# Encoder layer with mLSTM: scores, weights and scaled operands of each chunk formed beside the value projection and kept in DRAM

## Chip, cores and metric

One core of a Trainium2 chip runs the whole layer in one launch. The metric is device time in microseconds; a program's time is the median of its runs.

## The reference

1280 tokens of width 1024 in two sequences (256 and 1024 tokens, 2 and 8 chunks of 128) go through one layer, in float32. A norm and one input projection give pooled channels, and queries, keys, values, output gates and gates of an mLSTM with 4 heads of 128. It scans chunks in both directions; in one direction, per chunk and head:

```python
b = jnp.cumsum(fc, axis=-1)
logw = jnp.where(mask, b[..., :, None] - b[..., None, :] + ic[..., None, :], -jnp.inf)
m_row = jnp.maximum(b + m[..., None], jnp.max(logw, axis=-1))
s = jnp.einsum('bhjd,bhsd->bhjs', qc, kc) * jnp.exp(logw - m_row[..., None])
inter = jnp.exp(b + m[..., None] - m_row)
num = jnp.einsum('bhjs,bhsd->bhjd', s, vc) + inter[..., None] * jnp.einsum('bhed,bhjd->bhje', C, qc)
den = jnp.sum(s, axis=-1) + inter * jnp.einsum('bhd,bhjd->bhj', n, qc)
h = num / jnp.maximum(jnp.abs(den), jnp.exp(-m_row))[..., None]
# then C and n are decayed and gain u * v k and u * k
```

The heads of both directions are added, normed and gated; an output projection, a second norm, a router and 32 experts (top 2) and a last norm follow. Nothing of the latter is touched by the change.

## The kernel before

The five engines and their queues run programs of their own, ordered by semaphores; the order in each is written out by hand. The large products are made of three products of split operands (`product3`, L636 to L638).

The stages in order: norm and transposes of x; projections of 512, 512 and 256 tokens in the list `proj` (pooling, gates, output gates, keys, queries); then the values, one tile of 128 tokens at a time (`NPROJ + t`, 24 matmuls of 512 columns each); then the recurrence; then, per chunk, head norm, output projection and router; then the experts and the last norm. SP loads the slices of w_in through two slots of `w_st` (L403); each is split by ScalarE (L919) and VectorE (L1219).

The recurrence goes over `NU` = 40 units, two for each pair of heads in each of 10 steps, one for either direction `d`; `chunk_of` gives the chunk that a direction takes in a step. Per unit TensorE first does `unit_scores` for the unit after: two transposed key tiles (L728), two score tiles (L730), the mask and the negative row maximum brought into PSUM by products with selecting columns (L735, L736), and the factor of the state's part, `e_inter`, spread over the partitions in the same way (L738). ScalarE scales the keys (`uk`, L1044) and takes the exponential (`wgt`, L1052). VectorE multiplies scores and weights (`sT`, L1400) and scales the queries (`qi`, L1402). Then `unit_rows` on TensorE: state times queries and values times weighted scores (L751, L752), and what the state gains (L755, not in each sequence's last step). VectorE forms the denominator (L1413 to L1416), updates the state of two heads (L1419) and writes the pair's rows of `h_fb` (L1427). The next step of the same direction and pair is four units later. Meanwhile SP loads w_out slice by slice (L433), and ScalarE and VectorE split it after every fourth unit (L1058, L1440).

After the last unit (`h_done`, `NU`) SP loads what the output projection needs (L442 to L446). Each unit's tiles live in PSUM banks 4d to 4d + 3. GpSimd adds the two directions' h chunk by chunk (L567) and is idle otherwise.

Of the kernel before, what the change touches and what calls it, by code (L numbers as in the profile page):

```python
# [21 lines left out]
def build(nc, x_prompt, x_sample, norm1_g, w_in, pool_w, pool_scale, gate_b, head_norm_g, w_out,  # L22
# [28 lines left out]
    ogate_dram = nc.dram_tensor("ogateT", (MW, T), F32).ap()  # L51

# [18 lines left out]
    identb = const("identb", [P, P], BF16)  # L71
    maskb = const("maskb", [P, 2, P], BF16)
# [22 lines left out]
    row_picks = const("row_picks", [P, 8], F32R)  # L95
    e_inter = const("e_inter", [P, T], F32R)
    negm = const("negm", [P, T], F32R)
# [46 lines left out]
    dn = at("dn", X0 + 77 * KB, [P, 2, 2], F32)  # L144
    rdn = at("rdn", X0 + 77 * KB + 64, [P, 2, 2], F32)
    wo_lo = at("wo_lo", W0, [P, KD, D], F32R)
    uk = at("uk", V0, [P, 2, 2, P], F32)
    wgt = at("wgt", V0 + 2 * KB, [P, 2, 2, P], F32)
    sT = at("sT", V0 + 4 * KB, [P, 2, 2, P], F32)
    qi = at("qi", X0 + 77 * KB + 128, [P, 2, 2, P], F32)  # L150
# [58 lines left out]
    with ctx:  # L209
# [3 lines left out]
        def sem(name):  # L213
# [19 lines left out]
        g_abs, g_exp, g_ln, rows_ready, turned, dec_ready, cols_done, v_ones, state_zero, e_inter_exp, e_inter_hi, e_inter_done = (  # L233
            sem(n) for n in ("g_abs", "g_exp", "g_ln", "rows_ready", "turned", "dec_ready", "cols_done", "v_ones",
                             "state_zero", "e_inter_exp", "e_inter_hi", "e_inter_done"))

        kq_ready, nm_ready, uk_done, wgt_done, s_done, qi_done, kv_ready, rdn_done, state_done, h_done = (
            sem(n) for n in ("kq_ready", "nm_ready", "uk_done", "wgt_done", "s_done", "qi_done", "kv_ready", "rdn_done", "state_done", "h_done"))
# [14 lines left out]
        chosen_done, rank_ready, slots_done, count_ready, rounds_done, wexp_done, wts_done = (  # L253
            sem(n) for n in ("chosen_done", "rank_ready", "slots_done", "count_ready", "rounds_done", "wexp_done",
                             "wts_done"))
# [12 lines left out]
        f_in = [sem(f"f_in{i}") for i in range(NT)]  # L268
# [15 lines left out]
        N_CONST = 10  # L284
# [58 lines left out]

        def complete_after(t):
# [4 lines left out]
        EARLY = NT - 4  # L349

# [39 lines left out]
        def _(sp):  # L390
# [37 lines left out]
            for i in range(KD):  # L428
                if i < 2:
                    sp.wait_ge(wlo_done, NSL)  # L430
                else:
# [3 lines left out]
            for i in range(4):  # L435
                sp.wait_ge(ev_out[i], 16 * len(ring[i::4]))
            sp.wait_ge(h_done, NU)
            sp.wait_ge(state_done, NU)
# [60 lines left out]
            for t in range(NT):  # L499
                for k in range(2):  # L500
                    sp.dma_start(f_y[:, t, k, :], y_dram[k * T + t * P:k * T + (t + 1) * P, :]).then_inc(f_in[t], 16)
# [7 lines left out]
        def _(pool):  # L509
# [19 lines left out]
            for tile, value in ((identb[:, :], 0.0), (maskb[:, :, :], 0.0), (laterb[:, :], 1.0),  # L529
                                (edge[:, :, :], 1.0)):  # L530
                pool.memset(tile, value).then_inc(pool_step, 1)
            pool.wait_ge(pool_step, 5)
            pool.affine_select(out=identb[:, :], in_=identb[:, :], compare_op=ALU.not_equal, fill=1.0, base=0,
                               pattern=[[-1, P]], channel_multiplier=1).then_inc(consts_done, 1)
            for d, sign in enumerate((1, -1)):
                pool.affine_select(out=maskb[:, d, :], in_=maskb[:, d, :], compare_op=ALU.is_ge, fill=MASKED, base=0,
                                   pattern=[[sign, P]], channel_multiplier=-sign).then_inc(consts_done, 1)
# [12 lines left out]
            pool.wait_ge(pool_step, 8)  # L550
# [12 lines left out]


# [67 lines left out]
        def _(pe):  # L632
# [8 lines left out]
            def picks(r):  # L641
                return row_picks[:, r:r + 1].broadcast_to([P, P])

# [63 lines left out]

            for t in range(NT):
                n = NPROJ + t
                if t == 0:  # L710
# [10 lines left out]
            def unit_scores(n):  # L721
                step, pair, d, ck = unit(n)
                tok = slice(ck * P, (ck + 1) * P)
                heads = (2 * pair, 2 * pair + 1)
                if n >= 2:
                    pe.wait_ge(qi_done, n - 1)
                for hh_, h in enumerate(heads):
                    pe.transpose(psum[:, 4 * d, hh_ * P:(hh_ + 1) * P], kT[:, h, tok], ident[:, :])  # L728
                for hh_, h in enumerate(heads):
                    last = pe.matmul(psum[:, 4 * d, (2 + hh_) * P:(3 + hh_) * P], kT[:, h, tok], qT[:, h, tok],  # L730
                                     start=True, stop=True)
                last.then_inc(kq_ready, 1)
                for hh_, h in enumerate(heads):
                    out = psum[:, 4 * d + 1, hh_ * P:(hh_ + 1) * P]
                    pe.matmul(out, identb[:, :], maskb[:, d, :], start=True, stop=False)  # L735
# [965 lines left out]
```

## Time and profile before

| | us |
|---|---|
| median of 3 runs | 1281.9 (1279.71 to 1282.23) |
| profiled execution | 1278.36 |
| its span, first to last instruction | 1276.6 |
| PE busy | 1155.9 (91%) |
| DVE busy | 876.0 (69%) |
| ACT busy | 686.2 (54%) |
| POOL busy | 178.9 (14%) |

The profile is one execution on the chip. PE is TensorE's matmuls, PEld its weight loads, DVE VectorE, ACT ScalarE, POOL GpSimd; SPq is an issue on SP's DMA queue. Durations of matmuls are modelled and overlap, so what one costs is read from the distance between starts. PEclk is the granted TensorE clock as a share of full speed.

### The profile page before, as it was taken

Reading aid. Unit: us, or ns where it says so; the run is one execution under the profiler, and the core shown is the slowest. Engines: PE = TensorE matmul, PEld = TensorE weight load, DVE = VectorE, ACT = ScalarE, POOL = GpSimd, SP = SyncE. Lnnn points to the kernel's source line nnn. Section 1 sums busy time; section 2 is a strip of 40 time slices with the busy share of each in tenths; the row PEclk is TensorE's granted clock in tenths of the full one; section 3 lists DMA queues with packets and bytes.
Section 4 is the critical chain, followed back from the end, with each engine's and each line's share of the span. In section 5 each row is a group of like instructions: output and inputs, shape, how many; then the busy total and the mean of one; then the engine's idle time right before and its main releaser. Section 6 shows DMA issues by size and latency. Waiting matters only on the chain.

```text
span 1276.6 us, 18695 instructions
## 1 busy us (share of the span) xinstructions
PE 1155.9 (91%) x6071; PEld 978.7 (77%) x6071; DVE 876.0 (69%) x1413; ACT 686.2 (54%) x1122; POOL 178.9 (14%) x255
## 2 busy tenths in 40 slices
PE   5999999999999989998399999999999999999920
PEld 4887888878899968887278788888888888888810
DVE  5649410010188836665488999999999999999958
ACT  5431331121265643323177887788778877887733
POOL 1100200000010200212211221222122212211100
PEclk9999999999999989998599999999999999999965
DMA  8112230110011063542579999999999999999757
GB/s 229 56 45 71 101 97 17 50 60 7 1 51 51 2 197 101 106 143 100 196 266 369 366 376 384 382 375 387 385 384 384 387 385 384 375 378 388 272 228 302
DMA packets 118115, 282.05 MB, mean 221 GB/s; under 512 B 22144, under 2 KB 53376, under 8 KB 118064
## 3 DMA queue, kind: packets, MB, share of 16 engines
q1 hardware_dynamic: 103600, 245.01, 53.1%
q0 software_dynamic: 14464, 36.37, 7.6%
q8 instruction: 31, 0.51, 0.2%
q14 instruction: 20, 0.16, 0.0%
HBM read 261.76 MB, written 32.68 MB: 231 GB/s over the span
## 4 chain that ended last, share of the span: by engine, by line
PE 50%; DVE 7%; ACT 4%; DMA 2%; issue 1%; ACTq 0%; POOL 0%; SPq 0%; POOLq 0%; DVEq 0%
PE psum L636 15%; PE psum L638 15%; PE psum L637 15%; DVE e_lo L1533 3%; ACT e_hi L1105 3%; PE psum L849 2%; PE psum L807 1%; PE psum L882 1%; DVE x L1660 1%; DVE x L1668 1%; DVE x L1658 1%; PE psum L796 1%; DMA gx<-xn_scratch,row_of 1%; DMA f_y<-expert_rows 0%; PE psum L775 0%
## 5 line engine op out<-in xcount | busy, mean ns | idle before, releaser
L1533 DVE TENSOR_TENSOR e_lo<-e_st,e_hi 128x1024 fp32r<-128x1024 f32 x384 | 442.4, 1218 | 16.0 <-ACT e_hi L1105 15.1
L1105 ACT ACTIVATE e_hi<-e_st 128x1024 fp32r<-128x1024 f32 x384 | 372.3, 1050 | 9.5 <-PE psum L638 9.1
L636 PE MATMUL psum<-e_hi,ex_hi 128*128 128x512 f32 x512 | 204.3, 399 | 8.9 <-DVE ex_lo L1580 3.7
L637 PE MATMUL psum<-e_lo,ex_hi 128*128 128x512 f32 x512 | 200.8, 392 | 0.0
L638 PE MATMUL psum<-e_hi,ex_lo 128*128 128x512 f32 x512 | 200.7, 392 | 0.0
L636 PE MATMUL psum<-xT_hi,w_hi 128*128 128x512 f32 (+1 forms) x408 | 146.2, 358 | 6.4 <-DVE w_lo L1219 3.3
L638 PE MATMUL psum<-xT_hi,w_lo 128*128 128x512 f32 (+1 forms) x408 | 144.9, 355 | 0.0
L637 PE MATMUL psum<-xT_lo,w_hi 128*128 128x512 f32 (+1 forms) x408 | 144.8, 355 | 0.0
L636 PEld LDWEIGHTS psum<-e_hi,ex_hi 128*128 128x128 f32 x512 | 96.7, 189 | 42.0 <-DVE e_lo L1533 16.6
L638 PEld LDWEIGHTS psum<-e_hi,ex_lo 128*128 128x128 f32 x512 | 96.7, 189 | 20.9
L637 PEld LDWEIGHTS psum<-e_lo,ex_hi 128*128 128x128 f32 x512 | 96.8, 189 | 19.1
L1219 DVE TENSOR_TENSOR w_lo<-w_st,w_hi 128x1024 fp32r<-128x1024 f32 x21 | 25.6, 1222 | 121.3 <-ACT w_hi L919 121.3
L636 PE MATMUL psum<-e_hi,ht_hi 128*128 128x512 f32 x256 | 105.8, 413 | 1.3 <-DVE yo L1599 1.1
L638 PE MATMUL psum<-e_hi,ht_lo 128*128 128x512 f32 x256 | 100.4, 392 | 0.0
L637 PE MATMUL psum<-e_lo,ht_hi 128*128 128x512 f32 x256 | 100.0, 391 | 0.0
L636 PEld LDWEIGHTS psum<-xT_hi,w_hi 128*128 128x128 f32 x408 | 77.6, 190 | 18.0 <-DVE w_lo L1219 4.0
L638 PEld LDWEIGHTS psum<-xT_hi,w_lo 128*128 128x128 f32 x408 | 77.4, 190 | 10.9
L637 PEld LDWEIGHTS psum<-xT_lo,w_hi 128*128 128x128 f32 x408 | 77.5, 190 | 10.6
L603 POOL COPY row_to<-rows_to 128x1 int32 (+1 forms) x32 | 27.1, 848 | 416.9 <-DVE yo L1599 416.9
L636 PE MATMUL psum<-wo_hi,mix_hi 128*128 128x512 f32 x160 | 65.1, 407 | 1.2 <-DVE mix_lo L1458 1.2
L637 PE MATMUL psum<-wo_lo,mix_hi 128*128 128x512 f32 x160 | 63.2, 395 | 0.0
L638 PE MATMUL psum<-wo_hi,mix_lo 128*128 128x512 f32 x160 | 63.2, 395 | 0.0
(233 smaller groups left out, 1872.7 us busy)
## 6 DMA issues: line engine op xcount, KB each, us to landing
e_st<-in_expert_w_gate_dram SPq DMA_DIRECT2D x128, 512.0 KB, 5.8
e_st<-in_expert_w_up_dram SPq DMA_DIRECT2D x128, 512.0 KB, 6.8
e_st<-in_expert_w_down_dram SPq DMA_DIRECT2D x128, 512.0 KB, 8.6
w_st<-in_w_in_dram SPq DMA_DIRECT2D x20, 512.0 KB, 4.0
f_y<-expert_rows SPq DMA_DIRECT2D x20, 512.0 KB, 12.2
xn_scratch<-xn POOLq DMA_DIRECT2D x10, 512.0 KB, 3.4
out_dram<-x SPq DMA_DIRECT2D x10, 512.0 KB, 4.8
x_in<-in_x_sample_dram POOLq DMA_DIRECT2D x8, 512.0 KB, 5.2
```

Of the source, the lines that this page charges most:

```text
L603: pool.tensor_copy(row_to[:, b:b + 1], rows_to[:, bass.ds(i, 1)]).then_inc(row_placed, 1)
L636: pe.matmul(out, a_hi, b_hi, start=start, stop=False)
L637: pe.matmul(out, a_hi, b_lo, start=False, stop=False)
L638: return pe.matmul(out, a_lo, b_hi, start=False, stop=stop)
L796: last = pe.transpose(psum[:, 5 + k // 4, (k % 4) * P:(k % 4 + 1) * P], xn2[:, t % 2, k:D:KD], ident[:, :])
L807: last = pe.matmul(psum[:, 7, 0:NL], xn2T[:, k, :], rw[:, k, :], start=(k == 0), stop=(k == KD - 1))
L849: last = pe.transpose(psum[:, 2 + k // 4, (k % 4) * P:(k % 4 + 1) * P], gx[:, b, k:D:KD], ident[:, :])
L882: last = pe.transpose(psum[:, 6, k * P:(k + 1) * P], hh[:, k:F:KF], ident[:, :])
L1105: act.activation(e_hi[:, r, :, :], e_st[:, slot, :, :], ACT.Copy).then_inc(ehi_done, 1)
L1219: dve.tensor_tensor(w_lo[:, m % 4, :, :], w_st[:, m % 2, :, :], w_hi[:, m % 4, :, :].bitcast(F32), ALU.subtract).then_inc(wlo_done, 1)
L1533: dve.tensor_tensor(e_lo[:, r, :, :], e_st[:, slot, :, :], e_hi[:, r, :, :].bitcast(F32), ALU.subtract).then_inc(elo_done, 1)
L1658: link(dve.scalar_tensor_tensor(out=x1[:, t, :], in0=f_y[:, t, 0, :], scalar=wts[:, 0, t:t + 1], in1=x1[:, t, :], op0=ALU.mult, op1=ALU.add))
```

## The change

Scores, weights, scaled keys and scaled queries no longer belong to a unit. They are formed in 20 blocks, one for each chunk and pair of heads with both directions in it, while TensorE projects the values: two blocks' transposes and scores stand ahead of each value tile from the second on. The negative maxima and the state's factors are written to DRAM as rows, and each block's rows are read back broadcast over 128 partitions. GpSimd masks them, ScalarE adds the bias and takes the exponential, VectorE multiplies. One of three buffers `blk` holds a block (128 x 1536 floats), which SP stores in `units_dram`. The recurrence loads each unit's 128 x 768 floats from there: the first four into the place of xT_lo, the others into eight slots that lie over qT and kT. A unit on TensorE is `unit_rows` alone, with four banks for rows and four for gains; units of a sequence's first step leave the state product out. ScalarE writes `h_fb`; VectorE's small steps are laid between its state updates. Columns of the gates are formed before the first keys are taken. The constants for masking and selecting by TensorE go.

```diff
     ogate_dram = nc.dram_tensor("ogateT", (MW, T), F32).ap()
+    negm_dram = nc.dram_tensor("neg_max_rows", (2 * H, T), F32).ap()
+    inter_dram = nc.dram_tensor("inter_rows", (2 * H, T), F32).ap()
...
+    blk = [at(f"blk{i}", off, [P, 2, 3, 2, P], F32) for i, off in enumerate((V0, top_rows, W0 + 32 * KB))]
+    first_units = at("first_units", X0 + 40 * KB, [P, KD, T], F32)
+    units = at("units", Q0, [P, 8, 6, P], F32)
...
+            def block_in(i):
+                ck, pair = BLOCKS[i]
+                tok = slice(ck * P, (ck + 1) * P)
+                if i == 0:
+                    sp.wait_ge(rows_out, 64)
+                    for j in range(4):
+                        sp.wait_ge(ev_out[j], 16 * len(ring[j::4]))
+                elif i == 2:
                     sp.wait_ge(wlo_done, NSL)
...
+                elif i >= 3:
+                    sp.wait_ge(blk_out[i % 3], 16 * (i // 3))
+                for kind, rows, arrived in ((0, negm_dram, nm_in), (2, inter_dram, inter_in)):
+                    for d in range(2):
+                        sp.dma_start(blk[i % 3][:, d, kind, :, :],
+                                     rows[d * H + 2 * pair:d * H + 2 * pair + 2, tok].unsqueeze(0)
+                                     .broadcast_to([P, 2, P])).then_inc(arrived[i % 3], 16)
+            def block_out(i):
+                sp.wait_ge(s_done, i + 1)
+                sp.dma_start(units_dram[i].rearrange("p d n -> p (d n)"),
+                             blk[i % 3][:, :, :, :, :].rearrange("p d k h n -> p (d k h n)")).then_inc(blk_out[i % 3], 16)
+            def unit_load(n):
+                step, pair, d, ck = unit(n)
+                if n >= 12:
+                    sp.wait_ge(kv_ready, n - 7)
+                dst = first_units[:, 0:6, n * P:(n + 1) * P] if n < 4 else units[:, n % 8, :, :]
+                sp.dma_start(dst, units_dram[BLOCKS.index((ck, pair)), :, d, :]
+                             .rearrange("p (k n) -> p k n", n=P)).then_inc(unit_in[n % 8], 16)
+            def wo_in(i):
+                if i >= 2:
                     sp.wait_ge(wolo_done, i - 1)
                 sp.dma_start(w_st[:, i % 2, :, :].rearrange("p k n -> p (k n)"),
                              w_out[0, i * P:(i + 1) * P, :]).then_inc(wo_load[i % 2], 16)
...
+            for i in range(3):
+                block_in(i)
+            for i in range(NB):
+                block_out(i)
+                if i + 3 < NB:
+                    block_in(i + 3)
+                if i == NB // 2:
+                    sp.wait_ge(proj_ready, NPROJ + 4)
+                    for n in range(4):
+                        unit_load(n)
+            for j in range(3):
+                sp.wait_ge(blk_out[j], 16 * len(range(j, NB, 3)))
+            for n in range(4, 12):
+                unit_load(n)
+                if n == 4:
+                    wo_in(0)
+                    wo_in(1)
+            for n in range(12, NU):
+                unit_load(n)
+                if n % 4 == 0 and 2 <= n // 4 - 1 < KD:
+                    wo_in(n // 4 - 1)
...
+            for i in range(NB):
+                pool.wait_ge(nm_in[i % 3], 32 * (i // 3 + 1))
+                for d, sign in enumerate((1, -1)):
+                    logw = blk[i % 3][:, d, 0, :, :]
+                    ins = pool.affine_select(out=logw, in_=logw, compare_op=ALU.is_ge, fill=MASKED, base=0,
+                                             pattern=[[0, 2], [sign, P]], channel_multiplier=-sign)
+                ins.then_inc(masked, 1)
...
+            def block_scores(i):
+                ck, pair = BLOCKS[i]
+                tok = slice(ck * P, (ck + 1) * P)
+                if i == 0:
+                    pe.wait_ge(cols_done, 1)
+                    pe.wait_ge(act_took, act_results(NPROJ))
+                if i >= 4:
+                    pe.wait_ge(s_done, i - 3)
+                for hh_ in range(2):
+                    pe.transpose(psum[:, 4 + i % 4, hh_ * P:(hh_ + 1) * P], kT[:, 2 * pair + hh_, tok], ident[:, :])
+                for hh_ in range(2):
+                    last = pe.matmul(psum[:, 4 + i % 4, (2 + hh_) * P:(3 + hh_) * P], kT[:, 2 * pair + hh_, tok],
+                                     qT[:, 2 * pair + hh_, tok], start=True, stop=True)
+                last.then_inc(kq_ready, 1)
             for t in range(NT):
                 n = NPROJ + t
+                for i in range(max(2 * t - 1, 0), 2 * t + 1 + (t == NT - 1)):
+                    block_scores(i)
...
+                pe.wait_ge(unit_in[n % 8], 16 * (n // 8 + 1))
+                if n >= 4:
+                    pe.wait_ge(h_done, n - 3)
+                    pe.wait_ge(state_done, states_kept(n - 3))
+                for hh_ in range(2):
+                    h = 2 * pair + hh_
+                    out = psum[:, n % 4, hh_ * (P + 1):(hh_ + 1) * (P + 1)]
+                    if not from_zero(step):
+                        pe.matmul(out, unit_part(n, 2, hh_), state[:, d, h, :], start=True, stop=False)
+                    last = pe.matmul(out, unit_part(n, 0, hh_), v[:, ck, h, :], start=from_zero(step), stop=True)
                 if carries(step):
...
+                    for hh_ in range(2):
+                        last = pe.matmul(psum[:, 4 + n % 4, hh_ * (P + 1):(hh_ + 1) * (P + 1)], unit_part(n, 1, hh_),
+                                         v[:, ck, 2 * pair + hh_, :], start=True, stop=True)
                 last.then_inc(kv_ready, 1)
...
+            pe.wait_ge(s_done, NB)
...
+                        act.activation(inter_rows[0:64, :], g_e[:, :], ACT.Exp).then_inc(inter_done, 1)
+                        gate_columns()
...
+            def block_weights(i):
+                ck, pair = BLOCKS[i]
+                act.wait_ge(masked, i + 1)
+                for d in range(2):
+                    for hh_ in range(2):
+                        r = d * H + 2 * pair + hh_
+                        wgt = blk[i % 3][:, d, 0, hh_, :]
+                        ins = act.activation(wgt, wgt, ACT.Exp, bias=cols[:, ck, 0, r:r + 1])
+                ins.then_inc(wgt_done, 1)
+            block_weights(0)
+            for t in range(NT):
+                for i in range(2 * t + 1, min(2 * t + 3, NB)):
+                    block_weights(i)
+                v_part(t)
...
+                act.wait_ge(rdn_done, n + 1)
                 for hh_ in range(2):
...
+                    h = 2 * pair + hh_
+                    ins = act.activation(h_fb[:, d, ck, h * P:(h + 1) * P],
+                                         psum[:, n % 4, hh_ * (P + 1):hh_ * (P + 1) + P], ACT.Copy,
+                                         scale=rdn[:, n % 4, hh_:hh_ + 1])
+                ins.then_inc(h_done, 1)
...
+            def block_products(i):
+                ck, pair = BLOCKS[i]
+                tok = slice(ck * P, (ck + 1) * P)
+                keys = psum[:, 4 + i % 4, 0:2 * P].rearrange("p (h n) -> p h n", h=2)
+                scores = psum[:, 4 + i % 4, 2 * P:4 * P].rearrange("p (h n) -> p h n", h=2)
+                dve.wait_ge(inter_in[i % 3], 32 * (i // 3 + 1))
+                dve.wait_ge(kq_ready, i + 1)
+                qi = blk[i % 3][:, :, 2, :, :]
+                for d in range(2):
+                    dve.tensor_tensor(qi[:, d, :, :], qi[:, d, :, :], qT[:, 2 * pair:2 * pair + 2, tok], ALU.mult)
+                for d in range(2):
+                    r = d * H + 2 * pair
+                    dve.tensor_tensor(blk[i % 3][:, d, 1, :, :], keys,
+                                      cols[:, ck, 2, r:r + 2].unsqueeze(2).broadcast_to([P, 2, P]), ALU.mult)
+                dve.wait_ge(wgt_done, i + 1)
+                for d in range(2):
+                    ins = dve.tensor_tensor(blk[i % 3][:, d, 0, :, :], scores, blk[i % 3][:, d, 0, :, :], ALU.mult)
+                ins.then_inc(s_done, 1)
+            for i in range(NB):
+                block_products(i)
...
+                def keep(hh_):
+                    old = state[:, d, 2 * pair + hh_, :]
+                    return dve.scalar_tensor_tensor(out=old, in0=old, scalar=decay[:, r + hh_, step:step + 1],
+                                                    in1=gained[:, hh_, :], op0=ALU.mult, op1=ALU.add)
+                wait(dve, h_done, n - 3)
+                steps[0] += 2
+                dve.tensor_tensor(dn[:, n % 4, :], num[:, :, P], cols[:, ck, 1, r:r + 2], ALU.max).then_inc(dve_step, 1)
+                if carries(step) and from_zero(step):
+                    dve.tensor_copy(state[:, d, 2 * pair:2 * pair + 2, :], gained).then_inc(state_done, 1)
+                elif carries(step):
+                    keep(0)
+                dve.wait_ge(dve_step, steps[0] - 1)
+                dve.scalar_tensor_tensor(out=dn[:, n % 4, :], in0=num[:, :, P], scalar=-1.0, in1=dn[:, n % 4, :],
+                                         op0=ALU.mult, op1=ALU.max).then_inc(dve_step, 1)
+                if carries(step) and not from_zero(step):
+                    keep(1).then_inc(state_done, 1)
+                dve.wait_ge(dve_step, steps[0])
+                dve.reciprocal(rdn[:, n % 4, :], dn[:, n % 4, :]).then_inc(rdn_done, 1)
```

## Rows read from the trace of the kernel before

**Rows 1.** Windows: stretch, busy time of each engine, clock, DMA share, GB/s.

```profile
284.00:340.20 56.20, 56.20 (x240) 46.04 (x240) 0.00 (x0) 6.41 (x25) 0.00 (x0) 0.97 0.05 19
...
341.70:444.20 102.50, 101.66 (x920) 100.72 (x920) 84.98 (x311) 63.02 (x217) 12.67 (x8) 1.00 0.09 32
```

**Rows 2.** Timeline of one unit: start us, us, engine, line, operation.

```profile
370.80 0.38 PE L728 MATMUL psum<-ident,kT 128*128 128x128 f32 x2
...
371.00 0.16 DVE L1413 TENSOR_TENSOR dn<-psum,cols 128x2 f32<-128x2 f32 x1
371.02 0.61 PE L730 MATMUL psum<-qT,kT 128*128 128x128 f32 x4
371.20 0.16 DVE L1414 SCALAR_TENSOR_TENSOR dn<-psum,dn 128x2 f32<-128x2 f32 x1
...
371.47 0.22 PE L735 MATMUL psum<-maskb,identb 128*128 128x128 bf16 x1
...
371.48 0.59 DVE L1419 SCALAR_TENSOR_TENSOR state<-state,decay,psum 128x129 f32<-128x129 f32 x2
...
372.05 0.44 PE L751 MATMUL psum<-state,qi 128*128 128x129 f32 x2
...
372.99 0.61 PE L755 MATMUL psum<-v,uk 128*128 128x129 f32 x4
...
373.44 0.38 PE L728 MATMUL psum<-ident,kT 128*128 128x128 f32 x2
```

**Rows 3.** Groups of instructions from 200 to 560 us: busy us, mean ns.

```profile
L1052 ACT ACTIVATE wgt<-psum,cols 128x128 f32<-128x128 f32 x80 | 25.0, 364 | 0.0
...
L1400 DVE TENSOR_TENSOR sT<-psum,wgt 128x256 f32<-128x256 f32 x40 | 16.9, 423 | 14.6 <-ACT wgt L1052 14.2
...
L1440 DVE TENSOR_TENSOR wo_lo<-w_st,wo_hi 128x1024 fp32r<-128x1024 f32 x8 | 9.7, 1215 | 0.0
...
L1058 ACT ACTIVATE wo_hi<-w_st 128x1024 fp32r<-128x1024 f32 x8 | 8.4, 1055 | 0.0
```

**Rows 4.** Timeline of the SP queue's issues after the last h.

```profile
446.72 0.38 SPq L442 DMA_DIRECT2D mixf<-pooledT  x1
447.15 0.50 SPq L444 DMA_DIRECT2D og<-ogateT  x1
447.70 0.50 SPq L446 DMA_DIRECT2D x<-in_x_prompt_dram  x1
```

**Rows 5.** Issues of L504: landing, us from issue.

```profile
DMA to landing us min/median/max: 2.6/4.8/15.3
```

**Rows 6.** Windows: the experts' stage, columns as in the first group.

```profile
610.00:1230.00 620.00, 584.55 (x2706) 478.06 (x2706) 543.38 (x563) 451.39 (x541) 116.12 (x133) 0.97 0.94 353
```

**Rows 7.** Issues of L403, slices of w_in: landing.

```profile
DMA to landing us min/median/max: 3.7/4.0/9.7
```

**Rows 8.** Issues of L433, slices of w_out: landing.

```profile
DMA to landing us min/median/max: 3.1/3.2/4.3
```

**Rows 9.** The issue of L407, norm1_g broadcast: landing.

```profile
DMA to landing us min/median/max: 5.2/5.2/5.2
```

**Rows 10.** Groups of GpSimd.

```profile
L520 POOL TENSOR_SCALAR_AFFINE_SELECT ident<-ident 128x128 f32<-128x128 f32 x1 | 0.3, 284 | 0.2 <-POOL ident L518 0.2
```

**Rows 11.** Timeline before the value projection.

```profile
282.67 1.23 DVE L1219 TENSOR_TENSOR w_lo<-w_st,w_hi 128x1024 fp32r<-128x1024 f32 x1 [1.13 <-ACT w_hi L919]
...
283.92 0.84 SPq L433 DMA_DIRECT2D w_st<-in_w_out_dram  x2
```

**Rows 12.** Timeline of VectorE in the gate rows.

```profile
103.05 3.05 DVE L1345 SCALAR_TENSOR_TENSOR negm<-g_m,negm 32x1280 fp32r<-32x1280 f32 x3
```

**Rows 13.** Windows: clock around the first output projection.

```profile
449.00:450.00 1.00, 0.35 (x2) 0.00 (x0) 0.00 (x0) 0.44 (x2) 0.13 (x1) 0.50 1.44 332
...
457.00:458.00 1.00, 1.00 (x4) 0.71 (x4) 0.38 (x2) 0.00 (x0) 0.00 (x0) 0.50 1.08 342
...
459.00:460.00 1.00, 1.00 (x5) 0.78 (x5) 0.12 (x1) 1.00 (x3) 0.00 (x0) 1.00 0.63 231
```

More of the change, by code:

```diff
@@ L341, in unit, with states_kept @@
             return step, pair, d, chunk_of(step, d)
+        def states_kept(n):
+            return sum(carries(m // 4) for m in range(n))
         def complete_after(t):
@@ L349, in build, with from_zero @@
         EARLY = NT - 4
+        BLOCKS = [(c, pair) for c in sorted(range(NT), key=lambda c: min(s for s in range(NT) for b in range(2)
+                                                                          if chunk_of(s, b) == c)) for pair in range(2)]
+        NB = len(BLOCKS)
+        def from_zero(step):
+            return step in (0, C0)
         def carries(step):
@@ L717, in _ @@
                 last.then_inc(proj_ready, 1)
[L721 to L735, printed above, removed]
-                    pe.matmul(out, picks(d * H + h), negm[:, tok], start=False, stop=True)
-                for hh_, h in enumerate(heads):
-                    last = pe.matmul(psum[:, 4 * d + 1, (2 + hh_) * P:(3 + hh_) * P],
-                                     picks(d * H + h), e_inter[:, tok], start=True, stop=True)
-                last.then_inc(nm_ready, 1)
@@ L742, in unit_rows @@
             def unit_rows(n):
                 step, pair, d, ck = unit(n)
-                heads = (2 * pair, 2 * pair + 1)
-                pe.wait_ge(qi_done, n + 1)
-                if n >= 2:
-                    pe.wait_ge(h_done, n - 1)
-                    pe.wait_ge(state_done, n - 1)
-                for hh_, h in enumerate(heads):
-                    out = psum[:, 4 * d + 2, hh_ * (P + 1):(hh_ + 1) * (P + 1)]
-                    pe.matmul(out, qi[:, d, hh_, :], state[:, d, h, :], start=True, stop=False)
-                    last = pe.matmul(out, sT[:, d, hh_, :], v[:, ck, h, :], start=False, stop=True)
+                pe.wait_ge(unit_in[n % 8], 16 * (n // 8 + 1))
@@ L997, in _, with v_part @@
                 take(n)
[L1000 to L1012 removed]
+            def v_part(t):
                 act.wait_ge(proj_ready, NPROJ + t + 1)
@@ L1343, in gate_rows_stabilised @@
                 dve.wait_ge(list_set, 16)
[L1344 to L1350 removed]
+                by_direction(lambda r, o, i: dve.tensor_scalar(negm_rows[r, o], g_m[r, i], -1.0, None, ALU.mult))
                 dve.tensor_tensor(chunked(g_i), per_chunk(mprev), chunked(g_m), ALU.subtract)
@@ L1417, in heads_out @@
-                if carries(step):
-                    for hh_ in range(2):
-                        ins = dve.scalar_tensor_tensor(
-                            out=state[:, d, 2 * pair + hh_, :], in0=state[:, d, 2 * pair + hh_, :],
-                            scalar=decay[:, r + hh_, step:step + 1],
-                            in1=psum[:, 4 * d + 3, hh_ * (P + 1):(hh_ + 1) * (P + 1)], op0=ALU.mult, op1=ALU.add)
-                else:
-                    ins = dve.memset(state[:, d, 2 * pair:2 * pair + 2, :], 0.0)
```

174 lines of the change are left out of this document (51 added, 123 removed).

## Prediction

> **What bounds the kernel now.** I first cut the span into stretches with the table of windows, to see which engine fills each one [rows 1]. The value projection (284 to 340.2 us) and the recurrence (341.7 to 444.2 us) are both TensorE's: it is busy 56.2 of 56.2 us and 101.7 of 102.5 us. DMA is nearly idle in both (share 0.05 and 0.09), VectorE does nothing in the first and 85 us in the second. Then I read one unit of the recurrence in the timeline [rows 2], because modelled matmul durations overlap and only starts give the price. Transposes start at 370.80, scores at 371.02, mask and maximum at 371.47, rows at 372.05, state products at 372.99, the next unit at 373.44: one unit is 2.64 us, 40 of them are the 105 us from 341.7 to the last h near 446.6. So a change in this stage is worth what it takes out of TensorE's queue, until something else ends last.
>
> **What is taken away.** Everything between 370.80 and 372.05 leaves the unit: 1.25 us x 40 = 50 us. What stays is 0.94 us of rows and 0.45 us of state products, 1.39 us. The two first steps of the sequences lose the state product (0.47 + 0.45 = 0.92 us), the two last ones have no gain (0.94 us). TensorE needs 24 x 1.39 + 8 x 0.92 + 8 x 0.94 = 48 us. VectorE: the small operations start about 0.2 us apart when each waits for the last, the two state updates take 0.59 us together [rows 2]; laid into each other that is some 0.9 us a unit, with wo_lo 1.2 us in every fourth [rows 3]. ScalarE: two of about 0.3 us start to start, plus wo_hi 1.05 us per step and the squares. Both stay under 1.39 us a unit and four banks of PSUM cover their lag, so I cost them at nothing; without that cover it would be the 0.3 us by which four quick units are shorter than VectorE's four and a wo_lo, about 1 us in all.
>
> **What is added to TensorE.** A block's transposes and scores are 0.67 us by the starts above; 20 of them 13.4 us, beside the 56.2 us of 240 matmuls for the values [rows 1]. If TensorE set the pace, the stage would end near 354 us, and the whole would be 105 + 56 - 48 - 70 = 43 us faster. I don't think that it does.
>
> **What is added to the queues.** Each block needs four loads of 128 KB (rows broadcast to 128 partitions, in pieces of 512 B) and one store of 768 KB; each unit loads 384 KB. That is 10.5 + 15.7 + 15.7 = 42 MB that was not moved before. More important is SP's order: it issues the store of block i, then waits until that store has landed, then issues the four loads of block i + 3, and only then the store of block i + 1. Stores of successive blocks can't overlap, nor can the issues lie beside them. The three buffers don't help: one turn of this loop per block is the pace, whatever the engines do.
>
> The turn, term by term. Issues: three in a row on SP start 0.43 and 0.55 us apart [rows 4]; at 0.48 us four cost 1.9 us (bounds 4 x 0.36 = 1.45 and 4 x 0.55 = 2.2). Landing of the store: 512 KB to DRAM landed in 2.6 us at best [rows 5]. Bulk traffic moves 353 GB/s at share 0.94 [rows 6], 375 GB/s, so the further 262 KB cost 0.7 us: 3.3 us alone. The four loads stand ahead of it in the rings. Their work: slices of w_in in 512 B pieces land in 4.0 us, rows of 4 KB in 3.2 us [rows 7, 8], of which 0.2 us is the longer issue; so 512 KB in such pieces is 1.4 + 0.6 = 2.0 us. The one broadcast of before took 5.2 us, others beside it [rows 9], so up to 4.0 us. They are issued over 1.9 us and mostly gone when the store's data starts; I take 0.6 us of them (bounds 0 and 2.0). With two waits of 0.1 us: 1.9 + 3.3 + 0.6 + 0.2 = 6.0 us. Bounds: 1.45 + 3.3 = 4.75 us and 2.2 + 3.3 + 2.0 + 0.2 = 7.7 us. DMA work alone is 2.1 + 2.0 = 4.1 us, below the turn.
>
> The rest of a block's way is no bound. GpSimd's masks: 128 columns took 0.28 us [rows 10], 256 some 0.4, two 0.8 us. Exp: four of 364 ns, about 1.3 us. Products: six of 423 ns and about 0.35 apart, 2.1 us [rows 3]. From the last load's issue to the finished block some 5 to 8 us, against three turns (18 us) that it has. TensorE needs per two blocks 5.6 + 1.3 = 6.9 us of 12.
>
> **The sum.** Blocks 0 and 1 load while VectorE does the last w_lo, which ends at 283.9 us [rows 11], so the first block is done near 286.5. Turns follow at 6.0 us. After block 10 the four preloads of units (1.57 MB, 4.2 us) stand ahead of the next store: +4.2. The store of block 16 is issued at 286.5 + 96 + 4.2 = 386.7, lands at 390.6, the loads of block 19 are issued by 392.6, masked by 394.5, exponentiated by 395.9, multiplied by 397. The stage that ended at 340.2 now ends at 397: that is what is paid for 50 us.
>
> The recurrence starts at 397. Units 0 to 3 take 4 us. Units 4 and later lie over qT and kT, so they wait for the last store (3.3 us, 400.4) and a load of 384 KB (3.2 - 0.35 = 2.85 us): 403.3. From there bandwidth counts: 384 KB are 1.05 us, a slice of w_out 1.4 us. Two slices stand behind unit 4, so unit 11 is there at 403.3 + 2.8 + 7 x 1.05 = 413.5. The other 28 units and six slices take 28 x 1.05 + 6 x 1.4 = 37.8 us: 451.3. A step is 5.6 us of DMA against 5.56 us of TensorE, two bounds that nearly meet and make nothing good for each other; I add 2 us. The last unit's 0.94 us and the way to h_done (about 1.3 us: three small ones, then ScalarE in place of VectorE) end it at 455.6, against 446.6: +9 us. The recurrence is 58 us instead of 105, and all of it and more is spent before it.
>
> Small things: VectorE's gate chain loses the 3.05 us of the low halves of negm [rows 12], which lie beside dense projections; the small ScalarE columns move from behind the queries to ahead of the first keys, where four banks of PSUM (a result of 512 tokens takes TensorE some 5.5 us) cover them, and would cost their 2 us once if they didn't; fewer constants on GpSimd. Zero each. The way from h_done on is the same instructions. With the profiled execution of 1278.4 us this gives 1287.4 us; the median of the runs is 3.5 us above that execution, so I forecast 1291 us.
>
> **A rule against the change.** TensorE's clock was 0.50 from 449 us on, after it had sat mostly idle, stayed so through the dense matmuls to 458 and was 1.00 from 459 on [rows 13]: 1.2 GHz, then 2.4. In the new value stage it idles some 5 us in each two turns, and then about 15 us before the recurrence. Values at half speed for their first 4 to 5 us make about 8 us of 5.6, and with the scores that is still under 12 us: hidden. The Trainium skill (TensorE: Matmul & The Clock Gate, HAM oscillation) says that a kernel whose matmuls are short beside the DMA waits between them is put back to the low clock each time. The trace of before has only the one such place. By that rule a recurrence paced by loads could stay slow; by the row it recovers within 5 us of dense work.
>
> **Rivals.**
> - *Shorter turn (faster).* If the stores land at their best and issues cost 0.36 us, the turn is 4.75 us. 16 turns then give back 20 us: the recurrence starts at 377 and the whole is 11 us faster, 1271 us. For it: the best landings of before. Against: loads are always in the rings just ahead. It decides from a turn of 5.4 us down. Chance 0.20; a turn from there to 5.6 us, no change, 0.13.
> - *Longer turn.* 128 readers of one row as slow as in [rows 9], stores held behind them: turn 7.0 us, +17 us, 1308 us; at 7.7 us, 1320 us. Chance 0.20.
> - *Low clock in the recurrence.* At 1.2 GHz a unit's 1.39 us becomes at most 2.78 us: 24 x 1.4 us, about +33 us, 1324 us. Chance 0.07.
> - *The stage is TensorE's after all* (43 us faster) would need a turn of 3.4 us, under the best landing plus issues. Under 0.01, in the first rival.
>
> My own case, a turn of 5.6 to 6.6 us, has 0.40 and reaches from 1284 to 1301 us. Within 0.2% (2.6 us) is about what a measurement can't tell from no change. The range goes to the fast rival's value and into the long turn: 1271 to 1312 us, which leaves out 0.07 below and 0.13 above. Faster 0.20, same 0.13, slower 0.67.
>
> **What would show it.** SP's stores in the block stage evenly about 6 us apart, each followed by four loads; TensorE at half load there, waiting for VectorE's products, those for exp, those for GpSimd, those for DMA; last product near 397 us; unit loads back to back with DMA share over 0.9 through the recurrence; from h_done on nothing different. I am wrong if stores come every 5 us or less, if TensorE's clock is 0.5 through the recurrence, or if units wait for h_done and not for their load.

## The result, and the profile after

| | before | after |
|---|---|---|
| median of 4 runs | 1281.95 us (1279.71 to 1282.23) | 1315.76 us (1313.08 to 1319.38) |
| profiled execution, span | 1278.4 us, 1276.6 us | 1315.85 us, 1314.1 us |
| first store of a block | – | 289.98 us (forecast 286.5) |
| last product of the block stage | – | about 424.6 us (forecast 397) |
| last h | near 446.6 us | near 483.9 us (forecast 455.6) |

The changed kernel is slower: 1.0263 times before (1.0246 to 1.028), +34 us. The direction was forecast, the size was not: 1291 us was predicted and 1312 us was the top of the range. Of the rivals it is the longer turn, 1308 to 1320 us, that came about. The experiments ran beside the kernel before once more; its medians there lay between 1280.49 and 1281.33 us, and each ratio below is to the one measured beside it.

The page of the kernel after, its first lines:

```profile
span 1314.1 us, 18003 instructions
PE 1134.0 (86%) x5679; PEld 952.1 (72%) x5679; DVE 863.2 (66%) x1390; ACT 683.9 (52%) x1121; POOL 196.1 (15%) x290
...
PE 70%; DMA 10%; DVE 9%; ACT 5%; SPq 3%; issue 2%; ACTq 0%; POOL 0%; POOLq 0%; DVEq 0%
PE psum L717 21%; PE psum L719 20%; PE psum L718 20%; DMA mlstm_units<-blk 7%; DVE e_lo L1598 3%; ACT e_hi L1177 3%; PE psum L920 2%; SPq L473 2%; PE psum L878 1%; PE psum L953 1%; PE psum L827 1%; PE psum L826 1%; DVE x L1725 1%; DVE x L1733 1%; DVE x L1723 1%
```

A transfer stands in the chain that ended last with 7% of the span, about 90 us: the store of blocks, `mlstm_units<-blk`. The windows of the two stages, which answer to [rows 1] (stretch, busy time of each engine, granted clock, DMA share, GB/s):

```profile
290.00:350.00 60.00, 50.17 (x239) 41.70 (x237) 18.68 (x54) 13.25 (x43) 6.45 (x17) 0.90 0.53 180
...
384.00:424.60 40.60, 10.37 (x36) 8.25 (x36) 12.58 (x36) 9.81 (x32) 4.59 (x12) 0.58 0.58 198
...
428.00:445.00 17.00, 12.68 (x82) 12.30 (x82) 7.49 (x31) 7.21 (x20) 2.32 (x2) 0.79 0.95 363
445.00:483.80 38.80, 36.41 (x323) 36.05 (x321) 29.80 (x151) 30.30 (x116) 10.62 (x7) 1.00 0.84 316
```

The first and third row are parts of the block stage. Transfers never fill it (0.53 and 0.58). TensorE is full in its first part only, since its scores may run four blocks ahead:

```profile
290.00:322.00 32.00, 32.00 (x164) 26.95 (x163) 10.34 (x30) 7.07 (x23) 3.78 (x10) 0.97 0.54 178
```

From 322.6 us on it waits for finished blocks, at first 2.1 us, then mostly over 5 us. From 384 us on, with the last value tile (397.0 to 404.6 us) in it, TensorE works 10.4 of 40.6 us and no other engine more than 12.6. That is how a stage looks that is paced by an order of waits. The recurrence is the other way round: transfers at 0.95, then TensorE at 36.4 of 38.8 us.

The chain of waits, from the issue of one store to the landing of the next (start, duration, what):

```profile
319.54 4.87 DMA mlstm_units<-blk
324.41 0.02 issue
324.42 0.36 SPq L473
324.78 0.04 issue
324.82 0.47 SPq L473
325.30 0.04 issue
325.34 0.47 SPq L473
325.81 0.04 issue
325.85 0.47 SPq L473
326.32 0.04 issue
326.36 5.18 DMA mlstm_units<-blk
```

This is the loop that the prediction described, with no engine in it: the store lands, SP issues four loads (1.9 us), then the next store. Only the landing is longer, 4.9 to 5.2 us where 3.9 (3.3 + 0.6) was put. From the store at 297.57 to that at 362.05 are nine turns, 7.16 us each. All landings of the store (min, median, max), and who waited for what, by instruction (us in total, times, longest; the longest of GpSimd's waits, 118.5 us, lies before the first block):

```profile
DMA to landing us min/median/max: 3.4/5.2/6.8
```

```profile
POOL blk L642 <- DMA blk<-neg_max_rows: 238.1, 20, 118.5
ACT blk L1096 <- POOL blk L642: 105.3, 20, 12.9
DVE blk L1457 <- DMA blk<-inter_rows: 87.2, 17, 10.8
```

The minimum of 3.4 us is the last store, issued with neither loads nor another store just ahead of it: the 3.3 us of the prediction is confirmed, and the loads ahead add 1.8 us, not 0.6. Exp waits for the mask and the mask for its load, as forecast. VectorE, though, waits for the load of the state's factors, the last one issued, and never for exp. The way of the last block, with the columns of the chain above:

```profile
418.92 3.55 DMA blk<-inter_rows
422.46 0.02 issue
422.49 0.76 DVE blk L1457 x2
```

What moved inside one turn is seen when it is cut into single microseconds (columns as above; loads issued from 324.4, the store at 326.36):

```profile
326.00:327.00 1.00, 1.00 (x4) 0.81 (x3) 0.00 (x0) 0.00 (x0) 0.00 (x0) 0.50 0.49 138
327.00:328.00 1.00, 1.00 (x3) 0.72 (x3) 0.00 (x0) 0.00 (x0) 0.00 (x0) 0.50 0.60 147
328.00:329.00 1.00, 1.00 (x4) 0.80 (x3) 0.00 (x0) 0.05 (x1) 0.77 (x2) 0.50 0.79 216
329.00:330.00 1.00, 1.00 (x5) 0.80 (x4) 0.28 (x1) 1.00 (x4) 0.00 (x0) 0.81 1.07 438
330.00:331.00 1.00, 1.00 (x6) 0.81 (x5) 1.00 (x4) 0.23 (x1) 0.00 (x0) 1.00 0.85 348
```

The row loads drain at 138 to 147 GB/s here, until about 329 us; only then does most of the store's data go, at 438 and 348 GB/s. Counted in the time of the queue the loads cost 1.9 us of issues and 1.8 us of the store's landing, 3.7 us for 512 KB (142 GB/s), not the 2.0 us taken from slices of w_in, and they don't lie under their own issues.

The column ahead of the DMA share is the granted clock: 0.50 in the first microseconds of a value tile that stood behind a wait (1.2 GHz of 2.4), 1.00 again after 3 to 5 us of dense work. By the rule of the Trainium skill (TensorE: Matmul & The Clock Gate, HAM oscillation) short bursts between DMA waits fall back each time; here the trace agrees: from 326 us on the clock was at 0.50 after each of TensorE's waits of 2.1, 5.6, 5.3, 5.6, 12.0 and 5.4 us. It cost the stage nothing that shows, since no instruction of TensorE stands in the chain from 297.57 us to the end of the stage. The prediction said that the trace of before has only one such place. It has a second, behind a wait of 3.2 us ahead of the values:

```profile
286.00:287.00 1.00, 1.00 (x4) 0.78 (x3) 0.00 (x0) 0.00 (x0) 0.00 (x0) 0.50 1.02 373
```

### The profile page after: what moved, and what is told of

It is laid out like the page before. It is cut to its first block, busy times and chain, and to the rows that moved or that the text cites. A ratio compares the mean times of both kernels' runs of the same rounds, so it can differ in the third digit from the quotient of the medians.

```text
span 1314.1 us, 18003 instructions
## 1 busy us (share of the span) xinstructions
PE 1134.0 (86%) x5679; PEld 952.1 (72%) x5679; DVE 863.2 (66%) x1390; ACT 683.9 (52%) x1121; POOL 196.1 (15%) x290
## 4 chain that ended last, share of the span: by engine, by line
PE 70%; DMA 10%; DVE 9%; ACT 5%; SPq 3%; issue 2%; ACTq 0%; POOL 0%; POOLq 0%; DVEq 0%
PE psum L717 21%; PE psum L719 20%; PE psum L718 20%; DMA mlstm_units<-blk 7%; DVE e_lo L1598 3%; ACT e_hi L1177 3%; PE psum L920 2%; SPq L473 2%; PE psum L878 1%; PE psum L953 1%; PE psum L827 1%; PE psum L826 1%; DVE x L1725 1%; DVE x L1733 1%; DVE x L1723 1%
## 5 line engine op out<-in xcount | busy, mean ns | idle before, releaser
L1096 ACT ACTIVATE blk<-blk,cols 128x128 f32<-128x128 f32 x80 | 25.6, 390 | 105.3 <-POOL blk L642 105.3
L1457 DVE TENSOR_TENSOR blk<-blk,qT 128x256 f32<-128x256 f32 x40 | 15.2, 421 | 95.4 <-DMA blk<-inter_rows 87.2
## 6 DMA issues: line engine op xcount, KB each, us to landing
f_y<-expert_rows SPq DMA_DIRECT2D x20, 512.0 KB, 12.6
```

Source lines behind the costliest of these rows:

```text
L1096: ins = act.activation(wgt, wgt, ACT.Exp, bias=cols[:, ck, 0, r:r + 1])
L1457: dve.tensor_tensor(qi[:, d, :, :], qi[:, d, :, :], qT[:, 2 * pair:2 * pair + 2, tok], ALU.mult)
```

## The experiments

Two theories. **Order**: SP's fixed order (a store, its landing, loads, the next store) is the bound, and the work itself would fit into less time. **Rows**: 128 partitions that read one row of DRAM are slow, and that sets the landing. Against them, **pieces or count**: 512 B pieces, or four transfers instead of two, are what costs. Each kernel below starts from the changed one.

**e1_next_store_first.** The loads for a block's buffer are issued one block later, after the next store, so no load stands between two stores that are ready:

```diff
                 block_out(i)
-                if i + 3 < NB:
-                    block_in(i + 3)
+                if i >= 1 and i + 2 < NB:
+                    block_in(i + 2)
```

> Same work; only SP's order changes: the store of block i + 1 no longer waits for the landing of store i and the loads of block i + 3. Theory A (the turn of 7.15 us is serial: a landing of 5.2 us, of which 3.4 us is the store's own and 1.8 us is waiting behind the four loads in the rings, then four issues of 0.48 us): stores overlap, and the turn is then set by the way from a block's load issue to its product (7.1 us in the changed kernel) less the 1.9 us of issues that lie in it, some 5.2 us. 16 turns x 1.9 us = 30 us faster than the changed kernel, about 1285 us. Theory B (the stage is bound by DMA work or by slow stores, whatever the order): turn stays near 7 us, 1310 to 1316 us.

Measured: 1280.49 us, 0.9997 times before (0.9983 to 1.0012). The SP queue's waits, of the changed kernel and then of e1 (what, us in total, times, longest):

```profile
SPq L473 <- DMA mlstm_units<-blk: 82.1, 17, 5.6
```

```profile
SPq L479 <- DVE blk L1464: 36.5, 17, 5.9
```

Where SP waited 17 times for a store to land, it waits here for products. 35 us came back from the order of two lines, with the same transfers. That is 5 us more than was expected, and still the change is worth nothing: the recurrence's gain and the stage's loss now cancel.

**e2_two_loads** and **e3_rows_of_1kb.** The rows are kept block by block, so that both heads lie together. e2 loads a kind with one transfer of 256 KB in place of two of 128 KB; e3 keeps four transfers, and the pieces are 1 KB in both.

```diff
-    negm_dram = nc.dram_tensor("neg_max_rows", (2 * H, T), F32).ap()
+    negm_dram = nc.dram_tensor("neg_max_rows", (NT, 2, 2, 2, P), F32).ap()
...
-                    for d in range(2):
-                        sp.dma_start(blk[i % 3][:, d, kind, :, :],
-                                     rows[d * H + 2 * pair:d * H + 2 * pair + 2, tok].unsqueeze(0)
-                                     .broadcast_to([P, 2, P])).then_inc(arrived[i % 3], 16)
+                    sp.dma_start(blk[i % 3][:, :, kind, :, :].rearrange("p d h n -> p d (h n)"),
+                                 rows[ck, pair].rearrange("d h n -> d (h n)").unsqueeze(0)
+                                 .broadcast_to([P, 2, 2 * P])).then_inc(arrived[i % 3], 16)
```

> Rows lie in DRAM block by block, so each block takes two loads of 256 KB in place of four of 128 KB, in 1 KB pieces; bytes and order are unchanged. Theory A with a price per load: 0.95 us of issues go and the rings drain sooner, landing of the store 5.2 to about 4.3 us, turn 5.3 us, about 1287 us. If only the issues count: turn 6.2 us, about 1301 us. Theory A with a price per byte read from one row by 128 partitions: what the issues save the store waits longer, turn 6.9 us, 1312 us. Theory B: 1310 to 1316 us.

> As the two-load version, but four loads of 128 KB as in the changed kernel: only the pieces grow from 512 B to 1 KB. If the pieces' number is what holds the rings: landing of the store 5.2 to about 4.4 us, turn 6.3 us, about 1302 us. If it is bytes or the number of loads: turn 7.1 us, 1315 us.

Measured: e2 1312.69 us, 1.0236 (1.0207 to 1.0265); e3 1311.11 us, 1.0212 (1.0182 to 1.0242). Landings of the store between 303 and 395 us, e2, then e3:

```profile
DMA to landing us min/median/max: 5.6/6.2/6.8
```

```profile
DMA to landing us min/median/max: 5.1/5.2/7.5
```

e2 saves 1.0 us of issues and pays 1.0 us of landing: the loads take their time whether SP is still issuing or already waiting. e3 changes nothing of the turn (7.2 us). Pieces and count are out.

**e4_no_factor_loads.** The rows of state factors are loaded only for the first three blocks; later blocks take what lies in the buffer, so this kernel leaves out their true factors.

```diff
-                for kind, rows, arrived in ((0, negm_dram, nm_in), (2, inter_dram, inter_in)):
+                for kind, rows, arrived in ((0, negm_dram, nm_in), (2, inter_dram, inter_in))[:2 if i < 3 else 1]:
...
-                dve.wait_ge(inter_in[i % 3], 32 * (i // 3 + 1))
+                dve.wait_ge(inter_in[i % 3], 32) if i < 3 else dve.wait_ge(masked, i + 1)
```

> Leaves out the loads of the state factors (two of four per block) after the first three blocks; the scaled queries of those blocks are then formed from what lies in the buffer. Theory A: two issues less (0.95 us), and the store waits about 0.9 us less behind loads: landing about 4.2 us, turn about 5.3 us, about 1286 us. Theory B (a store lands in 5.2 us by itself): landing stays, turn 6.2 us, about 1301 us.

Measured, one run: 1288.11 us, stores 5.6 us apart in the SP queue's timeline:

```profile
303.90 0.47 SPq L479 DMA_DIRECT2D mlstm_units<-blk  x1
...
309.53 0.47 SPq L479 DMA_DIRECT2D mlstm_units<-blk  x1
```

Half the loads and bytes take some 1.5 us out of a turn (1.0 of issues, 0.5 of landing), less than the 1.9 us expected. Against e2, which also issues two loads but of twice the bytes, the landing falls from 6.1 to 4.7 us: that part is the bytes'.

**e5_stores_from_gpsimd** and **e6_gpsimd_two_loads.** GpSimd issues the stores from its own queue, the store of block i - 2 ahead of the mask of block i; SP keeps the loads. e6 has the two loads of e2 too.

```diff
             for i in range(NB):
-                block_out(i)
                 if i + 3 < NB:
...
             for i in range(NB):
+                if i >= 2:
+                    block_out(i - 2)
                 pool.wait_ge(nm_in[i % 3], 32 * (i // 3 + 1))
```

> GpSimd issues the stores on its own queue (store i - 2 ahead of mask i); SP keeps the loads and their waits. Theory A now reads: row loads run at about 140 GB/s whatever their shape, 3.7 us a block, and a store in the same queue waits for them. In two queues they can run side by side: the turn is then what a buffer's round takes by three, some 7.1 us to the product and 4 us of landing, 3.8 us, or at the least 3.7 us of loads; with friction 4.5 us. Against the version with the next store first (5.0 to 5.6 us) 16 x 0.8 = 13 us less, about 1267 us. If loads and stores only share one capacity (3.7 + 2.1 us): no gain on it, 1280 us or more.

> Stores from GpSimd and two loads of 256 KB per block in 1 KB pieces in place of four. The loads' drain did not change with their number, so the same as with four loads (within 3 us) if the drain sets the pace; up to 15 us faster if SP's issues do.

Measured: e5 1276.34 us, 0.9962 (0.9948 to 0.9976); e6 1275.74 us, 0.9952 (0.9933 to 0.9971). The stores no longer stand behind loads: they land in 4.2 and 4.1 us (median). Both beat the kernel before by less than half a per cent. e5 is 9 us short of what was expected: its last store is issued at 384.1 us, its stores are 5.1 us apart on average. The mask still waits for its row load (SP issues it when a store has landed), so the slow loads stay in the way of a block; e8 tests that.

**e7_each_its_own_row.** The changed kernel in its own order, but each partition reads its own 512 B piece of another array (stored output gates); this kernel leaves out the true maxima and factors. One run, for the turn.

```diff
-                                     rows[d * H + 2 * pair:d * H + 2 * pair + 2, tok].unsqueeze(0)
-                                     .broadcast_to([P, 2, P])).then_inc(arrived[i % 3], 16)
+                                     ogate_dram.rearrange("(a p) t -> p a t", p=P)[:, 2 * d:2 * d + 2, tok]
+                                     ).then_inc(arrived[i % 3], 16)
```

> Changed kernel with its own order; the four loads of a block have the same bytes and 512 B pieces, but each partition reads a row of its own (of the stored output gates) in place of one row read by all 128: leaves out the true maxima and factors. If the one address is what slows the row loads: each drains in about 0.4 us, the store lands in 3.4 to 3.8 us, turn 5.5 us, the last product near 395 us of the span (424.6 in the changed kernel). If it is the piece or the load's own size: landing stays 5.2 us, turn 7.1 us. The total is not read, since the experts' lists change with the data; the stage's end is.

Measured (landings between 306 and 400 us, then two stores in the timeline):

```profile
DMA to landing us min/median/max: 3.6/4.0/6.9
```

```profile
306.80 0.47 SPq L479 DMA_DIRECT2D mlstm_units<-blk  x1
...
313.11 0.46 SPq L479 DMA_DIRECT2D mlstm_units<-blk  x1
```

Same number of transfers, bytes and pieces, other addresses: the landing falls from 5.2 to 4.0 us and the turn from 7.16 to 6.03 us (six turns from 306.80 to 343.00), not to the 5.5 us expected of this run. It is the turn of the prediction, term by term: 0.6 us behind the loads, 3.4 us alone. What this can't separate is the one address from the small region of DRAM in which all rows lie: here the pieces come from rows 5 KB apart.

**e8_a_copy_for_each** and **e9_copies_own_order.** GpSimd copies both kinds of rows 128 times in DRAM before the stage (5 MB each, two transfers), and each partition loads its own copy. e8 is e6 with this, e9 is e2 with this, in the changed kernel's own order.

```diff
+            for k, (dst, src) in enumerate(((negm_copies, negm_dram), (inter_copies, inter_dram))):
+                pool.wait_ge(rows_stored[k], 64)
+                pool.dma_start(dst.rearrange("q c r d h n -> q (c r d h n)"),
+                               src.rearrange("c r d h n -> (c r d h n)").unsqueeze(0)
+                               .broadcast_to([P, 8 * T])).then_inc(copied, 16)
...
-                                 rows[ck, pair].rearrange("d h n -> d (h n)").unsqueeze(0)
-                                 .broadcast_to([P, 2, 2 * P])).then_inc(arrived[i % 3], 16)
+                                 rows[:, ck, pair].rearrange("q d h n -> q d (h n)")).then_inc(arrived[i % 3], 16)
```

> The version with GpSimd's stores and two loads a block, and before the blocks each kind of row is copied 128 times in DRAM (5.2 MB each, issued by GpSimd after its mixer stores, while TensorE projects keys and queries), so that each partition reads a copy of its own. If one address for all partitions is what slows the row loads (3.7 us a block against some 2 us), the turn falls from 4.9 to 4.1 us, where 2.1 us of store and 2.0 us of loads fill the DMA engines: 16 x 0.8 = 13 us less than the version it is made from, about 1263 us. Rival: the copies themselves read one address 128 times, 37 us each, and delay the slices of w_in or the first block: no gain or a loss against 1276 us.

> The changed kernel's own order on SP (store, wait for its landing, loads), with two loads a block as in the two-load version (1312.7 us), but from 128 copies in DRAM. Serial turn: 3.4 us of store and some 2 us of loads, 5.4 us in place of 7.1: 16 x 1.7 = 27 us less, about 1286 us. If the address is not what matters: 1312 us.

Measured: e8 1266.13 us, 0.9882 (0.9863 to 0.990); e9 1287.41 us, 1.0062 (1.0038 to 1.0087). e8 is 1.2% faster than the kernel before, the first gain above half a per cent and the fastest version here; 1263 and 1286 us were expected. The copies didn't delay the first block, as the rival in the expectation had it: the first store is issued at 287.9 us, in e6 at 287.6. From its page (KB each, us to landing) and its windows:

```profile
mlstm_units<-blk POOLq DMA_DIRECT2D x20, 768.0 KB, 4.2
...
neg_max_copies<-neg_max_rows POOLq DMA_DIRECT2D x1, 5120.0 KB, 19.0
```

```profile
290.00:350.00 60.00, 56.23 (x298) 47.51 (x296) 28.13 (x78) 17.84 (x58) 14.70 (x34) 1.00 0.85 293
```

Against the changed kernel's 50.2 of 60 us at clock 0.90 TensorE is busy 56.2 at 1.00, and transfers have gone from 180 to 293 GB/s. The loads alone, in one microsecond before the store's data, of e2 and then of e9:

```profile
307.00:308.00 1.00, 1.00 (x6) 0.84 (x5) 0.00 (x0) 0.00 (x0) 0.00 (x0) 1.00 0.95 198
```

```profile
310.00:311.00 1.00, 1.00 (x7) 0.79 (x6) 0.00 (x0) 0.00 (x0) 0.00 (x0) 1.00 0.96 281
```

At the same busy share of the DMA engines the copies come at 281 GB/s and the single rows at 198.

All stages side by side, from the SP or GpSimd timelines. The turn is (last store - first store) / 19, preloads included. "Loads' cost" is the issues of one block, 1.9 us for four, 0.9 for two, plus what the median landing exceeds 3.4 us; it is given only where loads stand ahead of each store. Times of e4 and e7 are of one run with other data, which change the experts' lists.

| kernel | first, last store | turn | landing | loads' cost | time |
|---|---|---|---|---|---|
| after | 290.0, 424.6 | 7.1 | 5.2 | 3.7 | 1315.76 |
| e2 | 286.2, 417.9 | 6.9 | 6.1 | 3.6 | 1312.69 |
| e3 | 289.9, 425.8 | 7.2 | 5.2 | 3.7 | 1311.11 |
| e4 | 286.1, 399.2 | 6.0 | 4.7 | 2.2 | 1288.11 |
| e7 | 287.6, 401.3 | 6.0 | 4.0 | 2.5 | 1290.24 |
| e9 | 287.2, 397.7 | 5.8 | 4.7 | 2.2 | 1287.41 |
| e1 | 287.4, 390.5 | 5.4 | 5.0 | – | 1280.49 |
| e5 | 286.6, 384.1 | 5.1 | 4.2 | – | 1276.34 |
| e6 | 287.6, 383.3 | 5.0 | 4.1 | – | 1275.74 |
| e8 | 287.9, 375.1 | 4.6 | 4.2 | – | 1266.13 |

The time follows the last store: from after to e8 they fall together, by 49.5 us (424.6 to 375.1) and 49.6 us (1315.76 to 1266.13), and in every other row the two differences agree within 6 us. Both theories hold, but their prices can't be added, since each cure takes part of the other's gain. The stores' own queue is worth 37 us with slow rows (e2 to e6) and 21 us with copies (e9 to e8); copies are worth 25 us in the old order (e2 to e9) and 10 us where the stores have their own queue (e6 to e8). Together they are 47 us (e2 to e8), not 62.

## Why the prediction was right in direction and wrong in size

**What bounds the stage: right.** SP's loop, with the store's landing in it, paces the blocks; DMA work and engines don't. e1 and e5 show it by changing nothing but the order and the queue.

**Store alone, 3.3 us: right.** 3.4 us for the one store with nothing ahead. Issues 1.9 us: right.

**The step that failed: "I take 0.6 us of them (bounds 0 and 2.0)".** The loads cost 3.7 us with their issues, so the store waits 1.8 us behind them. The rate was taken from slices of w_in, which each partition reads from its own place. The row that did show a broadcast [rows 9] was the truer neighbour; it was used as the upper bound alone. e7 shows that the arithmetic was right for own addresses (0.6 us, turn 6.03), e2 and e3 that neither piece size nor the number of transfers makes up the rest, e4 beside e2 that bytes do. Turns of 7.16 us in place of 6.0, and 6.5 in place of 4.2 us for the preloads of units, 5.0 of them on their four issues (the gap from the store at 362.05 to that at 382.84 was 20.8 us, two turns of 7.16 and 6.5), make 16 x 1.16 + 2.3 = 21 us; the turns that varied make it 22 us.

**First store, forecast 286.5 us: 3.5 us late.** The last slice of w_in was issued at 280.6 us, where before it was 277.7, and w_lo ended at 287.2 instead of 283.9 [rows 11]. In eight of the nine experiments the first store is issued 2 to 4 us earlier, so this is at least in part a matter of one execution. The last block's way, from the issue of the store of block 16 to the last product, was 12.3 instead of 10.3: +2 us. Together: 3.5 + 22 + 2 = 27.5 us of the 27.6 by which the last product was late.

**The recurrence, 58 us: right in size, wrong in what paces it.** It ran from 424.6 to 483.9 us, 59 us, in place of 105. Units were forecast to wait for their loads all through; they did so twice (start, duration, in brackets the idle time before an instruction and what ended it):

```profile
431.54 0.49 PE L826 MATMUL psum<-state,units 128*128 128x129 f32 x2 [1.20 <-DMA units<-mlstm_units]
...
435.81 0.80 PE L826 MATMUL psum<-state,units 128*128 128x129 f32 x2 [3.12 <-DMA units<-mlstm_units]
```

From 435.8 us to its last product near 481.5 TensorE sets its own pace, 1.34 us a unit where 1.39 was put, and transfers are at 0.84, not above 0.9. The size came out all the same because the two bounds of a step were forecast within 0.1 us of each other; that part is luck of the numbers, not a right reading. At the end stands a term that was put at nothing, ScalarE's squares for the head norm, 2.3 us ahead of the last h:

```profile
480.01 2.33 ACT h_fb L1110 x16
482.34 1.53 ACT h_fb L1123 x6
```

The last h came 2.4 us after the last product, 1.3 us were forecast.

The low-clock rival happened in part. The clock was 0.50 at the start and again from 436 to 442 us, behind the wait of 3.1 us, with TensorE busy all the time; from 443 us on it was 1.00 to the end. A window, and the distance between starts of the same pair of matmuls at either level:

```profile
440.00:441.00 1.00, 1.00 (x7) 1.00 (x6) 0.18 (x2) 0.62 (x2) 0.00 (x0) 0.50 1.04 405
```

```profile
439.19 0.43 PE psum L827 x2
...
445.52 0.22 PE psum L827 x2
```

At 0.43 in place of 0.22 us the 6.4 us from 435.8 us on cost at most some 3 us, an estimate from the two rows, not the 33 us of the rival: the clock came back and stayed, as the row of before [rows 13] had it.

**The rest: right.** From the last h to the end of the span 830.2 us, before 830.0: the same instructions in the same time.

**The whole sum.** The profiled execution is 28.4 us above the 1287.4 us forecast for it: 27.6 us of the block stage, 0.7 of the recurrence, 0.2 of the rest. The medians are only 24.8 us apart, because 3.5 us were added for a median above the profiled execution, and this time the median lay 0.1 us below it. The nearest test of the sum is e9, loads from own addresses in the kernel's own order: its last store is issued at 397.7 us (last product forecast at 397) and it takes 1.0062 times before (forecast 1291 of 1281.95, 1.0071). Part of that agreement is chance, since e9 has two loads in place of four, with 1.0 us less of issues and a landing of 4.7 in place of 3.9 us. e7, which has the four loads, issues its last store at 401.3 us, 113.7 us after its first, where 110.5 were forecast.

## What to carry to other kernels

When a queue both stores and loads through one ring of buffers, write its order down as a cycle (issue, wait, issue) and sum it before looking at any engine's busy time; three buffers buy nothing if the queue waits for the last landing before it goes on. Moving a wait one step later, or giving stores to another engine's queue, was worth 35 to 39 us here, all that the change had lost. And take the rate of a load from a row with the same addresses: a broadcast to 128 partitions is no neighbour of a slice.

## What the runs showed of the hardware

- 128 partitions that read the same 512 B or 1 KB of DRAM got 138 to 147 GB/s in the turn shown (four loads) and 198 GB/s in the microsecond shown of e2 (two loads), where the DMA engines were 0.95 busy; a block's rows cost 3.6 to 3.7 us of the queue. From own addresses the same bytes cost 2.5 us in four loads (e7, 1.9 of it issues) and 2.2 us in two (e9, 0.9 of it issues).
- One transfer that copied 40 KB of rows 128 times within DRAM took 19.0 us for 5 MB, 276 GB/s, although it has one source as well. Why a broadcast is fast in this form and slow into the 128 partitions was not tried and stays open.
- A transfer behind others in one queue waits for their data, not for their issue: halving the number of issues (e2) moved 1.0 us from issue to landing and left the turn within 0.2 us.
